# Group A of a hybrid decoder step: the values stand in the array and the softmax weights move

## The chip, the cores and the metric

The kernel runs on one core of one Trainium2 chip. The time is the device time of one launch in microseconds (us); a smaller number is better. TensorE (PE in the rows) multiplies, with its weight loads listed apart as PEld; VectorE is DVE, ScalarE is ACT, GpSimd is POOL, and SyncE (SP) issues all DMAs.

## The reference

Two layers run over 1024 prompt tokens and 8 sample tokens, in float32. Each layer projects the normalised rows with one combined matrix and splits the columns among two groups of eight heads of 64 columns. Group A is dilated window attention, group B a matrix memory. Gated feed-forward and an embedding gate follow. The change touches group A on the prompt tokens:

```
for (window, dilation) in ((128, 1), (512, 4), (2048, 16)):
    s = einsum('qhd,khd->hqk', q, k) * 64 ** -0.5      # masked to the pattern, causal
    m = max(s, axis=-1);  e = exp(s - m);  l = sum(e, axis=-1)
    o = einsum('hqk,khd->qhd', e, v) / l
merged = sum(w * o) / sum(w),   w = l * exp(m - max over patterns of m)
```

The kernel computes the three patterns as one softmax: one mask over all 1024 keys holds for each pair of tokens the logarithm of how many patterns contain it. So for each head, output = (sum over keys of e times v) / (sum over keys of e).

## The kernel before

Five engines run programs written out by hand, tied by counting semaphores. `wait_ge` on an engine holds everything that stands behind it in that engine's program.

**Group A.** The eight heads are taken as four pairs p (`PAIRS`), and each pair in 16 units u (`UNITS`, `NU`): query block qb = u // 2 of 128 tokens, and head e = u % 2 of the pair. A unit works on the keys of blocks 0 to qb. Its steps, on bank names of the PSUM tensor `ps`:

- `scores(p, qb)` (L884, TensorE, once for both heads, at odd units, one query block ahead): queries stand, keys move, a head in each half of the array's rows, into banks 0 to 3.
- `masked(p, u)` (L1692, VectorE): adds the mask, takes the row maximum and writes to one of two buffers in `att` (L1700); L1702 makes the negated maximum. It stands one unit ahead.
- `probabilities(p, u)` (L1328, ScalarE): exponential in place (L1333).
- `turn_p(p, u)` (L899, TensorE): each 128x128 block of the weights is transposed (L910) to bank 4, blocks from the fifth on to bank 5.
- `near` (L1705, VectorE, L1711) and `evac_far` (L1336, ScalarE, L1345) copy these banks to one of two further buffers in `att`. Both wait until the values of two units before have been multiplied, since the buffer alternates with the unit.
- `values(p, u)` (L913, TensorE, L923): the turned block stands, 128 keys by 128 queries, and 65 columns of `zt` move, the 64 value columns of the head and a column of ones whose product is the sum of weights. The result is 128 queries by 65 in bank 6. It stands one unit late.
- `outputs(p, u)` (L1713, VectorE): reciprocal of the 65th column (L1718), then the product into `yb` (L1719).

A float32 product is two records in the trace, a transposition one. Between these steps TensorE has `products` for the next pair's projection (L783 to L785; `FILL` gives 8 or 4 steps of three matmuls a unit, and none in units 14 and 15), and `turn_third` (L869), which transposes three tiles of normalised queries or keys through bank 6, and so waits for that bank to be read. ScalarE's `z_evac` (L1305 to L1309) takes a finished tile of products out of PSUM; in its program it stands ahead of the exponential of the same unit. VectorE normalises the next pair's queries and keys in parts (`norm_part`: L1602 to L1629), and `y_squares` adds squares of the outputs. At SP, `store_y` waits for `o_read` and stores `yb`.

Group B, the output projection, the feed-forward and the embedding gate follow, and are not touched.

## Time and profile before

| | us |
|---|---|
| runs of the kernel before | 3622.18, 3626.34, 3626.39; median 3626.34 |
| the profiled execution | 3619.83 |
| its span, first to last instruction | 3618.0 |
| TensorE busy | 3345.3 (92% of the span) |
| VectorE busy | 2166.6 (60%) |
| ScalarE busy | 883.3 (24%) |
| GpSimd busy | 597.0 (16%) |

The profile is of one execution; its own time is 6.5 us under the median of the three runs. Group A of the first layer lies between about 118 and 475 us of the span, that of the second between about 1893 and 2250 us. Where the next matmul starts before the last has ended, the distance of two starts is what one costs, and not its duration.

### The profile page before, as it was taken

How to read it: one execution, taken by the hardware profiler on the slowest of the kernel's cores; microseconds unless marked ns; L12 is line 12 of the kernel's file. 1: busy time of each engine (PE TensorE's matmuls, PEld its weight loads, DVE VectorE, ACT ScalarE, POOL GpSimd, SP SyncE). 2: the span in 40 equal slices, each digit the busy share in tenths (PEclk: the TensorE clock that was granted, in tenths of full speed). 3: DMA queues.
4: the chain of work that ended last, by engine and by line, in shares of the span. 5: the costliest groups of instructions: out<-in, count | busy, mean ns of one | idle time of the engine just before them, and what ended most of it. 6: DMA issues, size and time to landing. Idle time of an engine off the chain costs nothing. (4 is left out here: it accounts for less than half of the span.)

```text
span 3618.0 us, 49560 instructions
## 1 busy us (share of the span) xinstructions
PE 3345.3 (92%) x19817; PEld 3076.7 (85%) x19817; DVE 2166.6 (60%) x4644; ACT 883.3 (24%) x1661; POOL 597.0 (16%) x498
## 2 busy tenths in 40 slices
PE   4899999978999999999978989997899999999989
PEld 4777767668899999998977877775799999999988
DVE  5666456666655555557566665556666555555573
ACT  4233322213211211113233332232031111111131
POOL 2001111110322222221110011112012221221211
PEclk7999989959999999999989999997599999999999
DMA  4111112442211111110211111225211111111101
GB/s 141 39 36 42 42 47 74 92 134 66 70 47 36 59 47 36 59 47 18 84 41 47 45 42 51 58 64 170 73 60 36 47 47 47 47 47 47 39 30 63
DMA packets 208269, 209.69 MB, mean 58 GB/s; under 512 B 34596, under 2 KB 180964, under 8 KB 205936
## 3 DMA queue, kind: packets, MB, share of 16 engines
q1 hardware_dynamic: 208040, 206.53, 19.2%
q8 instruction: 157, 2.57, 0.3%
q14 instruction: 72, 0.59, 0.1%
HBM read 175.03 MB, written 31.64 MB: 57 GB/s over the span
## 5 line engine op out<-in xcount | busy, mean ns | idle before, releaser
L767 POOL TENSOR_TENSOR wlo<-raw,whi 128x512 fp32r<-128x512 f32 (+3 forms) x488 | 596.2, 1258 | 2964.4 <-ACT whi L1257 2964.4
L783 PE MATMUL ps<-hi,wlo 128*128 128x344 f32 x2880 | 931.8, 324 | 25.7 <-DVE wb L2077 15.5
L784 PE MATMUL ps<-lo,whi 128*128 128x344 f32 x2880 | 925.1, 321 | 0.0
L785 PE MATMUL ps<-hi,whi 128*128 128x344 f32 x2880 | 924.7, 321 | 0.0
L783 PEld LDWEIGHTS ps<-hi,wlo 128*128 128x128 f32 x2880 | 546.2, 190 | 29.0 <-DVE wb L2077 16.1
L784 PEld LDWEIGHTS ps<-lo,whi 128*128 128x128 f32 x2880 | 545.7, 189 | 0.6
L785 PEld LDWEIGHTS ps<-hi,whi 128*128 128x128 f32 x2880 | 545.8, 190 | 0.0
L783 PE MATMUL ps<-whi,lo 128*128 128x512 f32 (+5 forms) x1152 | 462.3, 401 | 40.7 <-POOL wlo L767 25.7
L784 PE MATMUL ps<-wlo,hi 128*128 128x512 f32 (+5 forms) x1152 | 436.4, 379 | 0.0
L785 PE MATMUL ps<-whi,hi 128*128 128x512 f32 (+5 forms) x1152 | 436.4, 379 | 0.0
L2089 DVE TENSOR_TENSOR X<-X,ps 128x344 f32<-128x344 f32 x528 | 268.6, 512 | 196.0 <-PE ps L785 195.4
L783 PE MATMUL ps<-yhi,wlo 128*128 128x344 f32 x1056 | 339.7, 322 | 0.6 <-DVE X L2089 0.6
L785 PE MATMUL ps<-yhi,whi 128*128 128x344 f32 x1056 | 338.3, 320 | 0.0
L784 PE MATMUL ps<-ylo,whi 128*128 128x344 f32 x1056 | 337.3, 319 | 0.0
L783 PEld LDWEIGHTS ps<-whi,lo 128*128 128x128 f32 (+1 forms) x1152 | 215.1, 187 | 119.1 <-issue 61.3
L1483 ACT ACTIVATE wb<-wb 128x344 f32<-128x344 f32 x132 | 64.9, 492 | 847.5 <-DVE wb L2060 847.5
L785 PEld LDWEIGHTS ps<-whi,hi 128*128 128x128 f32 (+1 forms) x1152 | 214.0, 186 | 39.2
L784 PEld LDWEIGHTS ps<-wlo,hi 128*128 128x128 f32 (+1 forms) x1152 | 215.7, 187 | 32.0
L1257 ACT ACTIVATE whi<-raw 128x2048 fp32r<-128x2048 f32 (+3 forms) x122 | 214.0, 1766 | 53.2 <-DMA raw<-in_w_down 41.4
L1305 ACT ACTIVATE zt<-ps,rcol 128x256 f32<-128x256 f32 x144 | 68.1, 473 | 566.5 <-PE ps L785 429.3
L783 PEld LDWEIGHTS ps<-yhi,wlo 128*128 128x128 f32 x1056 | 198.6, 188 | 1.6 <-DVE X L2089 1.2
L784 PEld LDWEIGHTS ps<-ylo,whi 128*128 128x128 f32 x1056 | 198.3, 188 | 0.0
(273 smaller groups left out, 4208.3 us busy)
## 6 DMA issues: line engine op xcount, KB each, us to landing
raw<-in_w_up SPq DMA_DIRECT2D x44, 1024.0 KB, 5.1
raw<-in_w_in SPq DMA_DIRECT2D x112, 256.0 KB, 4.6
raw<-in_w_down SPq DMA_DIRECT2D x22, 1024.0 KB, 4.9
kvb<-in_cache_win_k SPq DMA_DIRECT2D x48, 256.0 KB, 3.2
cache<-in_cache_win_v SPq DMA_DIRECT2D x36, 256.0 KB, 5.6
x_scratch<-X SPq DMA_DIRECT2D x8, 1032.0 KB, 7.2
X<-x_scratch SPq DMA_DIRECT2D x4, 2064.0 KB, 14.3
raw<-in_w_out SPq DMA_DIRECT2D x8, 1024.0 KB, 6.5
```

The source lines that it names most:

```text
L767: pool.tensor_tensor(out=wlo[:, s, r], in0=raw[:, s, r], in1=whi[:, s, r].bitcast(F32), op=ALU.subtract).then_inc(w_split, 1)
L783: nc.tensor.matmul(out, a_lo, b_hi, start=first, stop=False)
L784: nc.tensor.matmul(out, a_hi, b_lo, start=False, stop=False)
L785: return nc.tensor.matmul(out, a_hi, b_hi, start=False, stop=last)
L1257: do(nc.scalar.activation(whi[:, s, 0:used], raw[:, s, 0:used], ACT.Copy), w_hi, wait=False)
L1305: do(nc.scalar.activation(zt[0:m, z, t, 0:2 * P], src[:, 0:2 * P], ACT.Identity, scale=r), wait=False)
L1483: do(nc.scalar.activation(wb[:, col(c)], wb[:, col(c)], ACT.Gelu_apprx_tanh), gelu_done, wait=False)
L2089: do(v.tensor_tensor(out=x, in0=x, in1=ps[:, 5 + g % 3, 0:CH], op=ALU.add), dn_read, wait=False)
```

## The change

In `values(p, qb)`, now once for a query block and both heads, the 64 value columns of a head stand, head 0 in the left half of the array's columns and head 1 in the right half, and 128 columns of turned weights move. The result is turned: 64 columns of each head by 128 queries, in bank 6. `outputs_copied` on VectorE copies it to `oa` (which is the idle `Cst` buffer), `turn_back` on TensorE transposes it into the second quarter of bank 6, and `outputs` multiplies both heads by their reciprocals in one instruction. The column of ones is no longer used; the sums of weights come from the exponential's own accumulator (`accum_out`), into `dsum`.

The steps move too. `values` stands at even units behind `turn_p`, for the query block before; `turn_back` at odd units between two halves of the products, or behind `turn_p` where there are none. `turn_third` goes to the end of odd units. `near` and `evac_far` wait for the values of the query block before, both heads. The semaphores `o_ready` and `o_read` now count query blocks.

```diff
+        dsum = sb("dsum", [P, 3, 2], F32, mid)
+        oa = Cst[:, 0:P]
...
-                def values(p, u):
-                    e, qb = UNITS[u]
-                    g = NU * p + u
+                def values(p, qb):
+                    g = NU * p + 2 * qb + 1
                     pe.wait_ge(*at(pt0, g + 1))
                     if qb >= 4:
                         pe.wait_ge(*at(pt1, far(g + 1)))
-                    pe.wait_ge(*at(o_read, g))
-                    zc = VO + e * (HD + 1)
+                    pe.wait_ge(*at(o_read, NT * p + qb))
                     for kb in range(qb + 1):
-                        a = 2 * SEQ + (g % 2) * SEQ + kb * P
-                        mm = nc.tensor.matmul(ps[:, 6, 0:HD + 1], att[:, a:a + P], zt[:, p % 2, kb, zc:zc + HD + 1],
-                                              start=(kb == 0), stop=(kb == qb))
+                        for e in range(2):
+                            a = 2 * SEQ + e * SEQ + kb * P
+                            zc = VO + e * (HD + 1)
+                            mm = nc.tensor.matmul(ps[HD * e:HD * e + HD, 6, 0:P], zt[:, p % 2, kb, zc:zc + HD], att[:, a:a + P],
+                                                  start=(kb == 0), stop=(kb == qb))
                     mm.then_inc(o_ready, 1)
+                def turn_back(p, qb):
+                    pe.wait_ge(*at(oc_done, NT * p + qb + 1))
+                    nc.tensor.transpose(ps[:, 6, P:2 * P], oa[:, :], ident[:, :]).then_inc(ob_ready, 1)
...
+                        if part:
+                            evac = (q_evac, k_evac)[part[2]], 3 * part[0] + part[1] + 1
+                        before = (p, qb - 1) if qb else (p - 1, NT - 1)
                         half = (ahead(u) + ahead(u + 1)) // 2
                         products(p + 1, ahead(u), half)
-                        if part:
-                            pe.wait_ge(*at(o_read, NU * p + u - 1))
-                            turn_third(*part)
-                        products(p + 1, half, ahead(u + 1))
-                        turn_p(p, u)
-                        if part:
-                            pe.wait_ge(*at((q_evac, k_evac)[part[2]], 3 * part[0] + part[1] + 1))
-                        if u:
-                            values(p, u - 1)
-                        elif p:
-                            values(p - 1, NU - 1)
-                values(PAIRS - 1, NU - 1)
+                        if e == 0:
+                            if part:
+                                pe.wait_ge(*at(o_read, NT * p + max(qb - 1, 0)))
+                                turn_third(*part)
+                            products(p + 1, half, ahead(u + 1))
+                            turn_p(p, u)
+                            if before[0] >= 0:
+                                if part or u and turn_part(p, u - 1):
+                                    pe.wait_ge(*at(*evac))
+                                values(*before)
+                        else:
+                            if half == ahead(u + 1):
+                                turn_p(p, u)
+                            if before[0] >= 0:
+                                turn_back(*before)
+                            if half < ahead(u + 1):
+                                products(p + 1, half, ahead(u + 1))
+                                turn_p(p, u)
+                            if part:
+                                pe.wait_ge(*at(o_read, NT * p + qb))
+                                turn_third(*part)
+                values(PAIRS - 1, NT - 1)
+                turn_back(PAIRS - 1, NT - 1)
...
-                    do(nc.scalar.activation(s, s, ACT.Exp, scale=SCALE, bias=nm[:, g % 2:g % 2 + 1]), p_done, wait=False)
+                    do(nc.scalar.activation(s, s, ACT.Exp, scale=SCALE, bias=nm[:, g % 2:g % 2 + 1],
+                                             accum_out=dsum[:, g // 2 % 3, g % 2:g % 2 + 1]), p_done, wait=False)
...
-                        act.wait_ge(*at(o_ready, g - 1))
+                        act.wait_ge(*at(o_ready, NT * p + qb))
...
-                        if part and part[2] == 0:
+                        if part and part[2] == 0 and u % 2 == 0:
...
+                        if part and part[2] == 0 and u % 2:
+                            evac_third(part[0], part[1])
...
-                        dve.wait_ge(*at(o_ready, g - 1))
+                        dve.wait_ge(*at(o_ready, NT * p + UNITS[u][1]))
...
-                def outputs(p, u):
-                    e, qb = UNITS[u]
-                    dve.wait_ge(*at(o_ready, NU * p + u + 1))
-                    if u % NT == 0:
-                        dve.wait_ge(*at(yb_stored[u // NT], 16 * p))
-                    do(v.reciprocal(den[:, 1:2], ps[:, 6, HD:HD + 1]))
-                    do(v.tensor_scalar(yb[:, qb, e * HD:(e + 1) * HD], ps[:, 6, 0:HD], den[:, 1:2], None, ALU.mult), o_read)
+                def outputs_copied(p, qb):
+                    dve.wait_ge(*at(o_ready, NT * p + qb + 1))
+                    do(v.tensor_copy(oa[:, :], ps[:, 6, 0:P]), oc_done, wait=False)
+                def outputs(p, qb):
+                    if qb % 4 == 0:
+                        dve.wait_ge(*at(yb_stored[qb // 4], 16 * p))
+                    do(v.reciprocal(den[:, 0:2], dsum[:, (NT * p + qb) % 3, :]))
+                    dve.wait_ge(*at(ob_ready, NT * p + qb + 1))
+                    do(v.tensor_tensor(out=yb[:, qb, :].rearrange("p (e d) -> p e d", e=2), in0=ps[:, 6, P:2 * P].rearrange("p (e d) -> p e d", e=2),
+                                       in1=den[:, 0:2].unsqueeze(2).to_broadcast([P, 2, HD]), op=ALU.mult), o_read)
...
-                        part = turn_part(p, u)
-                        if part and part[2] == 1:
+                        part, (e, qb) = turn_part(p, u), UNITS[u]
+                        keys = part and part[2] == 1
+                        before = (p, qb - 1) if qb else (p - 1, NT - 1)
+                        if keys and e == 0:
                             evac_third(part[0], part[1])
+                        if e and before[0] >= 0:
+                            outputs(*before)
                         near(p, u)
-                        if u:
-                            outputs(p, u - 1)
-                        elif p:
-                            outputs(p - 1, NU - 1)
+                        if keys and e:
+                            evac_third(part[0], part[1])
+                        if e == 0 and before[0] >= 0:
+                            outputs_copied(*before)
...
+                outputs_copied(PAIRS - 1, NT - 1)
+                outputs(PAIRS - 1, NT - 1)
```

The remaining edits are the counts of the semaphores and the waits of `store_y`, `z_evac` and group B's first step, which now count query blocks.

TensorE at the end of the third pair, units 13 to 15, before. L910 is `turn_p`, L923 `values`, L895 `scores` of the next pair, L869 `turn_third`:

```order
L785 MATMUL ps<-whi,hi 8x384
L910 MATMUL ps<-ident,att 128x128 x7
L923 MATMUL ps<-zt,att 128x65 x7
L910 MATMUL ps<-ident,att 128x128 x8
L923 MATMUL ps<-zt,att 128x65 x7
L895 MATMUL ps<-kT,rstd 128x128 x2
L910 MATMUL ps<-ident,att 128x128 x8
L923 MATMUL ps<-zt,att 128x65 x8
L783 MATMUL ps<-whi,lo 128x512
```

The same place in the changed kernel. L913 is `turn_p`, L927 `values`, L872 `turn_third`, L898 `scores`, L934 `turn_back`:

```order
L788 MATMUL ps<-whi,hi 8x384
L913 MATMUL ps<-ident,att 128x128 x7
L872 MATMUL ps<-ident,zt 128x128 x3
L913 MATMUL ps<-ident,att 128x128 x8
L927 MATMUL ps<-att,zt 64x128 x14
L898 MATMUL ps<-kT,rstd 128x128 x2
L913 MATMUL ps<-ident,att 128x128 x8
L934 MATMUL ps<-ident,Cst 128x128
L786 MATMUL ps<-whi,lo 128x512
```

Two calls of `values` for one head (L923) have left the places behind unit 13's and unit 15's `turn_p`; `turn_third` now stands between the `turn_p` of units 13 and 14, and one call for both heads stands behind that of unit 14.

VectorE at the same place, before, from unit 14 on. L1700 and L1702 are `masked`, L1711 is `near`, L1718 and L1719 are `outputs`:

```order
L1700 ISA att,mx<-ps,mask 128x1024
L1700 ISA mx 128x1
L1702 TENSOR_SCALAR nm<-mx 128x1
L1711 COPY att<-ps 128x512
L1718 RECIPROCAL den<-ps 128x1
L1719 TENSOR_SCALAR yb<-ps,den 128x64
L1682 TENSOR_TENSOR rowr<-yb 128x512
L1686 TENSOR_REDUCE yt<-rowr 128x4
L1687 TENSOR_TENSOR ssq<-ssq,yt 128x4
L1700 ISA att,mx<-ps,mask 128x128
L1700 ISA mx 128x1
L1702 TENSOR_SCALAR nm<-mx 128x1
```

VectorE in the changed kernel, from unit 14 on. L1727 and L1729 are `masked`, L1738 is `near`, L1742 `outputs_copied`, L1748 and L1750 `outputs`:

```order
L1727 ISA att,mx<-ps,mask 128x1024
L1727 ISA mx 128x1
L1729 TENSOR_SCALAR nm<-mx 128x1
L1738 COPY att<-ps 128x512
L1742 COPY Cst<-ps 128x128
L1709 TENSOR_TENSOR rowr<-yb 128x512
L1713 TENSOR_REDUCE yt<-rowr 128x4
L1714 TENSOR_TENSOR ssq<-ssq,yt 128x4
L1727 ISA att,mx<-ps,mask 128x128
L1727 ISA mx 128x1
L1729 TENSOR_SCALAR nm<-mx 128x1
L1748 RECIPROCAL den<-dsum 128x2
```

The outputs of a unit stood behind `near`; now a copy stands there in even units, and in odd units the outputs stand ahead of `near`.

## Rows read from the trace of the kernel before

**Rows 1.** Window of group A, first layer: us, busy by engine, clock, DMA.

```profile
118.00:475.00 357.00, 327.39 (x2024) 273.98 (x2022) 217.56 (x562) 114.23 (x225) 35.87 (x32) 0.97 0.17 46
```

**Rows 2.** Timeline of TensorE, third pair's end: start, us, what.

```profile
371.91 0.93 PE L910 MATMUL ps<-ident,att 128*128 128x128 f32 x7
372.67 1.67 PE L923 MATMUL ps<-zt,att 128*128 128x65 f32 x14
374.18 1.04 PE L910 MATMUL ps<-ident,att 128*128 128x128 f32 x8
375.06 1.70 PE L923 MATMUL ps<-zt,att 128*128 128x65 f32 x14
...
377.56 1.14 PE L910 MATMUL ps<-ident,att 128*128 128x128 f32 x8 [0.38 <-ACT att L1333]
378.54 1.90 PE L923 MATMUL ps<-zt,att 128*128 128x65 f32 x16
380.25 0.47 PE L783 MATMUL ps<-whi,lo 128*128 128x512 f32 x1
```

**Rows 3.** Timeline of TensorE: transpositions among products, first layer, third pair.

```profile
344.01 0.49 PE L869 MATMUL ps<-ident,zt 128*128 128x128 f32 x3
344.26 0.42 PE L783 MATMUL ps<-whi,lo 128*128 128x384 f32 x1
344.52 0.34 PE L784 MATMUL ps<-wlo,hi 128*128 128x384 f32 x1
344.70 0.34 PE L785 MATMUL ps<-whi,hi 128*128 128x384 f32 x1
```

**Rows 4.** Timeline of TensorE in group B: half the array's columns, then all.

```profile
496.07 1.93 PE L1046 MATMUL ps<-rowr,ident 8*64 8x512 f32 x8
497.93 0.50 PE L783 MATMUL ps<-whi,lo 128*128 128x512 f32 x1
...
500.91 3.69 PE L1054 MATMUL ps<-rowr,ident 8*128 8x512 f32 x8
```

**Rows 5.** Timeline of the weight loads of the first line of rows 4.

```profile
496.98 0.14 PEld L1046 LDWEIGHTS ps<-rowr,ident 8*64 8x64 f32 x2 [0.29 <-issue]
```

**Rows 6.** Timeline of TensorE in group B: a change to half the rows and back.

```profile
512.65 0.40 PE L784 MATMUL ps<-wlo,hi 128*128 128x512 f32 x1
512.89 0.40 PE L785 MATMUL ps<-whi,hi 128*128 128x512 f32 x1
513.22 0.49 PE L1000 MATMUL ps<-rstd,kT 64*128 64x128 f32 x4
513.64 0.50 PE L783 MATMUL ps<-whi,lo 128*128 128x512 f32 x1
```

**Rows 7.** Timeline of ScalarE, third pair, unit 13.

```profile
372.11 0.47 ACT L1305 ACTIVATE zt<-ps,rcol 8x256 f32<-8x256 f32 x1 [5.22 <-PE ps L785]
...
372.86 1.15 ACT L1333 ACTIVATE att<-att,nm 128x1024 f32<-128x1024 f32 x1
```

**Rows 8.** Timeline of VectorE, third pair, unit 14.

```profile
376.25 0.69 DVE L1711 COPY att<-ps 128x512 f32<-128x512 f32 x1
```

**Rows 9.** Groups by line, shapes apart: count | busy us, mean ns | idle before.

```profile
L1719 DVE TENSOR_SCALAR yb<-ps,den 128x64 f32<-128x64 f32 x128 | 36.3, 284 | 4.5
L1885 DVE TENSOR_TENSOR yb<-ps,den 128x128 f32<-128x128 f32 x64 | 18.7, 292 | 2.2
L1711 DVE COPY att<-ps 128x128 f32<-128x128 f32 x16 | 4.7, 292 | 55.4 <-PE ps L910 55.4
L1424 ACT ACTIVATION_READ_ACCUMULATOR vectors<-vectors 64x1 f32 x2 | 0.4, 186 | 0.0
```

**Rows 10.** Waits of TensorE, 118 to 475 us: total us, times, longest.

```profile
PE ps L869 <- issue: 7.5, 5, 3.0
PE ps L895 <- DVE nm L1702: 5.3, 2, 3.5
```

**Rows 11.** Window of 3.4 us behind the longest of those waits (columns of rows 1).

```profile
163.20:166.60 3.40, 3.40 (x14) 3.30 (x14) 0.78 (x3) 0.99 (x2) 1.71 (x2) 0.50 0.46 127
```

More of the change, by code:

```diff
@@ L217 @@
     gz_abs=1, gz_ln=1, lf_done=1, gates_read=9, z_done=72, qk_norm=12, qk_ssq=12, qk_rs=12, turned=40, q_evac=20, k_evac=20,
-    s_ready=32, s_masked=64, p_done=64, t0_ready=64, t1_ready=32, pt0=64, pt1=32, o_ready=64, o_read=64,
+    s_ready=32, s_masked=64, p_done=64, t0_ready=64, t1_ready=32, pt0=64, pt1=32, o_ready=32, oc_done=32, ob_ready=32, o_read=32,
     o_exp=4, yb_done=4, yb_stored0=64, yb_stored1=112, z_stored0=384, z_stored1=384, gr_ready=1, rows_done=1, iw_done=4, gc_ready=1,
@@ L376, in build @@
             "z_done", "qk_norm", "qk_ssq", "qk_rs", "turned", "q_evac", "k_evac")]
-        s_ready, s_masked, p_done, t0_ready, t1_ready, pt0, pt1, o_ready, o_read = [sem(n) for n in (
-            "s_ready", "s_masked", "p_done", "t0_ready", "t1_ready", "pt0", "pt1", "o_ready", "o_read")]
+        s_ready, s_masked, p_done, t0_ready, t1_ready, pt0, pt1, o_ready, oc_done, ob_ready, o_read = [sem(n) for n in (
+            "s_ready", "s_masked", "p_done", "t0_ready", "t1_ready", "pt0", "pt1", "o_ready", "oc_done", "ob_ready", "o_read")]
         o_exp = sem("o_exp")
@@ L604, in store_y @@
                 def store_y(p, half):
-                    sp.wait_ge(*at(o_read, NU * p + NT * (half + 1)))
+                    sp.wait_ge(*at(o_read, NT * p + 4 * (half + 1)))
                     yv = Yd[half * 512:(half + 1) * 512, p * P:(p + 1) * P].rearrange("(t p) c -> p t c", p=P)
@@ L1024, in _ @@
                         pe.wait_ge(*at(pt1, far(NU * PAIRS)))
-                        pe.wait_ge(*at(o_read, NU * PAIRS))
+                        pe.wait_ge(*at(o_read, NT * PAIRS))
                         gate_rows()
@@ L1295, in z_evac @@
                         if p - 2 < PAIRS:
-                            act.wait_ge(*at(o_ready, NU * (p - 1)))
+                            act.wait_ge(*at(o_ready, NT * (p - 1)))
                         else:
@@ L1747, in _ @@
                             y_squares(p, rowr[:, :], slice(0, 4))
-                outputs(PAIRS - 1, NU - 1)
+                outputs_copied(PAIRS - 1, NT - 1)
+                outputs(PAIRS - 1, NT - 1)
                 y_squares(PAIRS - 1, rowr[:, :], slice(4, NT))
```

## The prediction

> **What bounds the kernel now.** I read the windows by stage first, then the timeline of TensorE inside a pair, then its waits, and last the other engines at the places where TensorE waits. In group A of the first layer TensorE is busy 327.4 of 357 us, VectorE 217.6, ScalarE 114.3, at a granted clock of 0.97 [rows 1]. So TensorE bounds the stage, but 29.6 us are idle, and where it idles another engine sets the pace. The waits name two kinds: `turn_third` for the normalised tiles (7.5 us, one of 3.0) and `scores` for the maxima (5.3 us, one of 3.5), both VectorE's work in the first half of a pair [rows 10]. In units 8 to 15 the blocks are many, and there TensorE's gaps are short.
>
> A third thing is seen only by laying two timelines beside each other. In unit 13 `turn_p` starts at 371.91 and that of unit 14 at 374.18 [rows 2]. The exponential that unit 14's needs starts at 372.86, takes 1.15 and ends at 374.01, 0.17 before; it starts so late since it stands behind the copy of the tile whose products ended just ahead of unit 13's `turn_p` [rows 7]. TensorE shows no gap there only because `values` of unit 12 fills it exactly. Work taken out of such a hole saves nothing.
>
> **What `values` costs now.** 2 layers, 4 pairs, 2 heads and 36 blocks with 2 records each are 1152 records of 65 columns. From start to the next line's start, 14 of them take 1.51 us (372.67 to 374.18) and 16 take 1.71 (378.54 to 380.25) [rows 2]: 0.107 us each. In all 123 us.
>
> **What it costs after.** A block needs two records for each head, 128 columns moving, 64 standing: again 1152 records. The question is whether the two halves run at once. The nearest rows say yes: line 1046 loads 64 columns into alternate halves and moves 512; 8 records take 1.86 us up to the next line (496.07 to 497.93), while line 1054, with all columns, takes 3.69 for 8 [rows 4]. Loads are hidden there too: the next pair's two loads take 0.14 beside the running matmuls [rows 5]. Of the 1.86, some 0.15 are loading and emptying (next part), so a step of two records is 0.43 for 512 columns and a fourth of that, 0.107, for 128; 576 steps cost 61.6 us. Saved: 61.6 us, if the halves are wholly parallel. The other end is no parallelism: 1152 times 0.107, nothing saved. I take the first, since rows 4 have the same order of instructions and the same halves; what they lack is that only 8 rows of the array are active and that both halves get the same moving data.
>
> A change of the array's shape costs something. Where products give way to the half-row form, the next start is 0.33 behind the last instead of 0.24, and the 4 records there take 0.42 (513.22 to 513.64) [rows 6], where two streams and one bare load of 0.107 make 0.32; the other 0.10 is emptying. Entering `values` therefore costs 0.10 and a bare load of half the columns, half of 0.107: 0.15, 64 times, 9.6 us. Leaving costs nothing new, as `scores`, itself in halves, stands behind it in both kernels; from halves of columns to halves of rows there is no row, between 0 and 0.2 each, and I take 0.05 (3 us), since both are already drained forms.
>
> The Trainium skill ("TensorE: Matmul & The Clock Gate", "The mechanism") says that weight loads overlap with matmuls in flight only when the row group differs. Rows 5 show loads into the same rows hidden, so I don't take it for the sum; by it every step would bare its load, which is the third rival.
>
> **`turn_back`.** 64 transpositions among products. Three such take 0.25 (344.01 to 344.26), and the product behind them 0.26 instead of 0.18 [rows 3]: one alone is 0.08 and 0.09, 0.17 us, so 10.9 us. Against it, 64 sections of old `values` at odd units go, each of which also made the product behind it 0.08 longer: 5.1 back. Gross for TensorE: 61.6 - 9.6 - 3 - 10.9 + 5.1 = 43 us.
>
> **VectorE and ScalarE.** The outputs of two units were two reciprocals and two multiplications of 0.284; now they are one reciprocal, a copy of 128 columns of 0.292 and one multiplication of 0.292 [rows 9]: about the same less one reciprocal a query block, off the path except in normalising units. There something new works the other way: `near` of an even unit waits for `values`, and its 0.4 to 0.7 us now stand behind it where they ran beside it. The reader of the accumulator costs ScalarE 0.186 [rows 9] 128 times, 24 us, hidden in its idle 240 us except where the exponential is waited for.
>
> **Where the gross saving goes.**
> - Unit 13 to 14, each pair. The hole of 2.27 us stays, as the exponential still starts behind the tile's copy; it grows by 0.19 for the reader. `values` of unit 12 (1.5) no longer fills it; `turn_third` (0.33), moved there, does in three pairs of four. Given back: 6 x 1.36 + 2 x 1.69 = 11.5 us.
> - Unit 14 to 15. `near` of unit 14 (0.69) [rows 8] starts only behind `values` (0.15 and 14 x 0.107), and unit 15's `turn_p` needs bank 4 from it: 0.88 + 1.65 + 0.69 and handovers of 0.2 are 3.42, against 3.38 now (374.18 to 377.56) [rows 2]. Where the exponential is late now, `near` is late next: nothing gained, nothing lost.
> - First halves of pairs, where VectorE and ScalarE set the pace [rows 10]: about 0.35 saved and hidden, and 0.35 added to VectorE's chain by the late `near`, in six pairs: 4 us.
> - The last pair of each layer has no products behind unit 15: `turn_back`, `outputs`, `near`, then the last `values` stand in a row, where the values of unit 14 covered `near`. 1.3 us; and copy, transposition and multiplication end the stage, 0.5 longer: 3.6 us together.
> - The clock. Behind the 3.0 us wait TensorE had the lower level, 1.2 GHz (0.50), for 3.4 us [rows 11]. One such stretch costs half its length. With new gaps of about 1 us I allow one or two more: 2 us.
>
> Sum: 43 - 11.5 - 4 - 3.6 - 2 = 22 us. The profiled execution of 3619.8 would be 3598; it stands 6.5 under the median of the runs, so from that median of 3626.3 the forecast is **3604**.
>
> **Rivals.**
> 1. More of the gross saving stays (3583 to 3593): the hole at unit 13 closes since ScalarE gets to the tile's copy earlier, or the first halves keep their savings. For it: 240 us of idle ScalarE a layer. Against: the copy waits for the products, and the order of its program is unchanged there.
> 2. Coupling goes deeper: VectorE, late in units 4 to 12 through `near` behind `values`, makes `turn_p` and `turn_back` wait, and gaps bring more clock stretches of 1.7 us. With 0.15 us more in each of 64 even units and three stretches, 9.6 + 5 us: about 3619. This is also the case that the change saves array time and no time.
> 3. The loads of halves are not hidden when the streams are as short as the loads. A bare load of 64 columns is 0.053, 576 times 31 us; 22 saved become 9 lost: 3635.
> 4. **Slower: the halves don't run at once.** With all 128 rows active, each half needs its own 128 rows of moving data, twice what any matmul of this trace reads; rows 6 run two halves of rows, which together read 128. If reads are the limit, a step costs 0.214 and the 61.6 us vanish, while changes of shape and `turn_back` stay: 3626 + 40 = 3666. It turns slower as soon as more than 22 of the 61.6 are missing, about a third of the overlap.
>
> **How the numbers follow.** Forecast (3595 to 3615) 0.60, rival 1 0.15, rival 2 0.10, rival 3 0.07, rival 4 0.08. The range of 3583 to 3625 holds the first three nearly whole and leaves out 0.17. A measurement of this kernel tells about 0.2%, 7 us, from no change. Faster by more: the forecast, rival 1 and a third of rival 2, 0.79. Within: the rest of rival 2 and a sliver of 3, 0.08. Slower: 0.13.
>
> **What would show it.** In the changed profile the 1152 records of `values` should lie in sections of 16 that take about 1.9 us, with pairs of starts some ns apart and 0.107 from pair to pair; 0.16 speaks for rival 3, 0.21 for rival 4. Unit 13's `turn_p` should again stand 2.3 to 2.5 us ahead of unit 14's, now with a gap of about a us that ends on the exponential. Unit 15's should wait for `near`. Group A should take about 10 us less a layer, nearly all of it behind unit 7 of each pair. The forecast is wrong if a stage other than group A changes, if `turn_back` shows waits for the copy, or if the clock in group A falls below 0.95.

## The result and the profile after

The changed kernel takes 3591.87 us in the median of four runs (3591.36 to 3593.18), the kernel before 3625.08 (3622.18 to 3626.39). The ratio is 0.991, with a 95% interval of 0.989 to 0.993: 33 us faster. The forecast was 3604 with a range of 3583 to 3625. The time lies inside, and 11 us more were saved than the 22 foreseen. The profiled execution took 3592.33, its span is 3589.7.

From the first start of `turn_p` to the last, group A took 333.08 us in both layers before. Now it takes 317.35 and 316.69, together 32.1 less, so the whole saving lies in group A. The spans of the two profiled executions differ by 28.3 only, since ahead of group A, where the code is the same, the changed one took 3.8 longer. The window of the first layer shows it (us, busy time of PE, PEld, DVE, ACT, POOL, clock, DMA share, GB/s), beside [rows 1]:

```profile
118.00:461.00 343.00, 310.63 (x2071) 244.16 (x2070) 201.52 (x534) 121.46 (x292) 35.56 (x32) 0.97 0.18 47
```

TensorE's busy time fell by 16.8 us there and the window by 14; the clock is the same 0.97. The timeline of TensorE at the third pair's end answers [rows 2] (start, us, what). The last three rows are the start of unit 0 of the fourth pair, with the largest section of `values`:

```profile
360.57 0.93 PE L913 MATMUL ps<-ident,att 128*128 128x128 f32 x7
361.33 0.49 PE L872 MATMUL ps<-ident,zt 128*128 128x128 f32 x3
362.81 1.09 PE L913 MATMUL ps<-ident,att 128*128 128x128 f32 x8 [0.99 <-ACT att L1357]
363.83 1.75 PE L927 MATMUL ps<-att,zt 128*64 128x128 f32 x28
365.51 0.49 PE L898 MATMUL ps<-kT,rstd 64*128 64x128 f32 x4
366.54 1.07 PE L913 MATMUL ps<-ident,att 128*128 128x128 f32 x8 [0.53 <-DVE att L1738]
367.44 0.27 PE L934 MATMUL ps<-ident,Cst 128*128 128x128 f32 x1
367.47 0.47 PE L786 MATMUL ps<-whi,lo 128*128 128x512 f32 x1
367.78 0.39 PE L787 MATMUL ps<-wlo,hi 128*128 128x512 f32 x1
...
373.12 0.27 PE L913 MATMUL ps<-ident,att 128*128 128x128 f32 x1
373.32 1.97 PE L927 MATMUL ps<-att,zt 128*64 128x128 f32 x32
375.22 0.70 PE L898 MATMUL ps<-kT,rstd 64*128 64x256 f32 x4
```

Read it in three steps. The 28 records of `values` take 1.68 us from start to the next line's start, and 32 take 1.90. Four more records, two pairs, cost 0.22, so a pair of records is 0.11, what one record cost before [rows 2]. In the trace the starts of single records lie 0.007 and 0.102 us apart in turn, 0.109 for a pair. Unit 13's `turn_p` stands 2.24 us ahead of unit 14's, where it stood 2.27, now with an open gap of 0.99 that ends on ScalarE's exponential. Unit 15's follows 3.73 behind, where it was 3.38, and ends on VectorE's `near`.

ScalarE at the same place (answering [rows 7]) still does the tile's copy before the exponential, and has the accumulator's reader behind it:

```profile
360.77 0.47 ACT L1329 ACTIVATE zt<-ps,rcol 8x256 f32<-8x256 f32 x1 [3.65 <-PE ps L788]
361.14 0.34 ACT L1333 ACTIVATE zt<-ps,rcol 8x128 f32<-8x128 f32 x1
361.51 1.15 ACT L1357 ACTIVATE att<-att,nm 128x1024 f32<-128x1024 f32 x1
362.57 0.19 ACT L1357 ACTIVATION_READ_ACCUMULATOR att<-att,nm 128x1 f32 x1
```

The waits of TensorE in group A, first layer (what waits, for whom: us in total, times, longest), answer [rows 10]:

```profile
PE ps L786 <- ACT zt L1333: 8.5, 20, 1.0
PE ps L872 <- issue: 4.9, 3, 2.2
PE ps L913 <- ACT att L1357: 4.5, 4, 1.6
PE ps L927 <- ACT zt L1345: 2.9, 1, 2.9
PE ps L913 <- DVE att L1738: 2.6, 4, 1.0
PE ps L927 <- ACT rstd L1345: 2.5, 1, 2.5
PE ps L927 <- DVE att L1738: 1.7, 1, 1.7
...
PE ps L898 <- DVE nm L1729: 0.7, 1, 0.7
PE ps L934 <- DVE Cst L1742: 0.4, 1, 0.4
```

`turn_back` (L934) waits once, for 0.4 us, in the last pair. The wait of `scores` for the maxima fell from 5.3 us [rows 10] to 0.7. New at the top are 20 waits of the products for a tile's copy (L1333). The kernel before had, in the same view:

```profile
PE ps L783 <- ACT zt L1309: 3.4, 7, 0.8
```

**Where in the pairs.** The starts of unit 0 and unit 8 split a pair. First layer, us before and after, from its 64 starts of `turn_p`:

| pair | units 0 to 7 | units 8 to the next pair |
|---|---|---|
| 1 | 42.5, 41.6 | 42.7, 38.5 |
| 2 | 43.2, 42.5 | 38.9, 35.7 |
| 3 | 46.2, 42.1 | 40.5, 37.1 |
| 4 | 45.1, 45.5 | 34.0, 34.3 (to unit 15) |

The second halves give 10.4 us, the first halves 5.3; in the second layer it is 10.4 and 6.0.

### The profile page after: what moved, and what is told of

It reads as the page before. It is cut to its first block and busy times, and to the rows that moved or that the text cites. A ratio compares the mean times of both kernels' runs of the same rounds, so it can differ in the third digit from the quotient of the medians.

```text
span 3589.7 us, 49644 instructions
## 1 busy us (share of the span) xinstructions
PE 3307.6 (92%) x19881; PEld 3014.6 (84%) x19881; DVE 2131.5 (59%) x4580; ACT 895.7 (25%) x1789; POOL 595.8 (17%) x498
## 5 line engine op out<-in xcount | busy, mean ns | idle before, releaser
L1738 DVE COPY att<-ps 128x512 f32<-128x512 f32 (+3 forms) x128 | 75.7, 592 | 220.4 <-PE ps L927 155.4
```

Source lines behind the costliest of these rows:

```text
L1738: do(v.tensor_copy(att[:, a:a + n], ps[:, 4, 0:n]), pt0, wait=False)
```

## Do the two halves run at once?

Three kernels change only what `values` does with the array. Each keeps the order of the steps of the changed kernel.

**One half of the array for both heads.**

```diff
-                    for kb in range(qb + 1):
-                        for e in range(2):
+                    for e in range(2):
+                        for kb in range(qb + 1):
...
-                            mm = nc.tensor.matmul(ps[HD * e:HD * e + HD, 6, 0:P], zt[:, p % 2, kb, zc:zc + HD], att[:, a:a + P],
+                            mm = nc.tensor.matmul(ps[0:HD, 6, 2 * P * e:2 * P * e + P], zt[:, p % 2, kb, zc:zc + HD], att[:, a:a + P],
```

> The changed kernel, but both heads' values stand in the left half of the array's columns, one head after the other, so no two streams can run at once; the outputs of the heads come out in the wrong places. Theory (the gain is that two halves stream at once, 0.107 us for a pair of records): the sections of values double, 0.107 for each record, 61.6 us more array time, of which little is hidden: 3645 to 3654 us. Rival (the halves never ran at once, the gain is from the new order of the steps): unchanged, 3590 to 3595.

It took 3653.37 us (3651.12 to 3655.31), 1.008 of the kernel before [1.0065, 1.0095]: 61.5 more than the changed kernel. Forecast for the whole overlap was 61.6. In the profiled executions 54.5 of it lie in group A and 5.0 where the code is the same, so that the two agree to a tenth is luck. TensorE's timeline, the same section of 32 records:

```profile
388.77 3.71 PE L927 MATMUL ps<-att,zt 128*64 128x128 f32 x32
392.41 0.49 PE L898 MATMUL ps<-kT,rstd 64*128 64x256 f32 x2
```

3.64 us instead of 1.90. The fourth rival (halves don't run at once) and the third (bare loads) fall with these two numbers, since 16 pairs of records at 0.21 or 0.16 make 3.4 or 2.6 us, where the changed kernel's take 1.7, and 0.2 for entering and leaving. The Trainium skill ("TensorE: Matmul & The Clock Gate", "The mechanism") says that loads overlap only where the row group differs. Here all rows are in use in both halves and the loads cost nothing beside the 0.109 of a pair; the measurement decides.

**Both halves, a head at a time.** The loops are exchanged, the halves kept:

```diff
-                    for kb in range(qb + 1):
-                        for e in range(2):
+                    for e in range(2):
+                        for kb in range(qb + 1):
```

> The changed kernel with each head in its own half, but all blocks of head 0 first and then all of head 1, where the change alternates. Theory (matmuls start in the order of the program, so two halves overlap only where neighbours differ in half): the overlap is lost but for one step a section, 0.107 for each record as with one half: 3640 to 3652 us. Rival (the queue of TensorE finds the other half's work further on): 3590 to 3600.

3635.61 us (3634.5 to 3638.24), 1.003 [1.0017, 1.004], 44 over the changed kernel and a little under the range expected of it. TensorE's timeline:

```profile
384.17 3.33 PE L927 MATMUL ps<-att,zt 128*64 128x128 f32 x32
387.43 0.70 PE L898 MATMUL ps<-kT,rstd 64*128 64x256 f32 x4
```

The section takes 3.26 us: of the 1.74 us that the halves saved, 0.38 are left. That is three and a half steps of 0.109, where the expectation had one. The sections by their number of records, us from start to the next line's start, say more:

| kernel | 4 | 8 | 12 | 16 | 32 |
|---|---|---|---|---|---|
| changed (alternating) | 0.37 | 0.59 | 0.81 | 1.02 | 1.90 |
| a head at a time | 0.37 | 0.59 | 1.07 | 1.51 | 3.26 |
| one half | 0.58 | 1.02 | 1.45 | 1.89 | 3.64 |

Up to four records of a head, nothing is lost by taking the heads in turn; beyond, 0.38 stays saved, however long the section. So in long sections the use of two halves isn't enough, and neighbours in the program should lie in different halves. But about four records of the second head do run beside the last of the first. The Trainium skill ("TensorE: Matmul & The Clock Gate", "Step-by-step: what each phase is for") says that matmuls stay in program order and only loads are pulled ahead. By a strict order of starts the halves would share one step of 0.109 in any section; from eight records on 0.38 to 0.43 are measured. The trace agrees with the page only in the main, and the measurement decides. The rows don't name the half of a record, so how the second head gets ahead is not shown.

**The new order of steps without the new product.** Weights stand and values move as before, for both heads in a row. There is no `turn_back` and no copy, and the sums come from the column of ones:

```diff
-                            mm = nc.tensor.matmul(ps[HD * e:HD * e + HD, 6, 0:P], zt[:, p % 2, kb, zc:zc + HD], att[:, a:a + P],
+                            mm = nc.tensor.matmul(ps[:, 6, P * e:P * e + HD + 1], att[:, a:a + P], zt[:, p % 2, kb, zc:zc + HD + 1],
...
-                            if before[0] >= 0:
-                                turn_back(*before)
```

> The order of the changed kernel with the arithmetic of the kernel before: turned weights stand, 65 columns move, both heads in a row at even units, no turning back, no accumulator. Theory (order alone is a loss of holes, halves are the gain): the sections double at even units, the values of unit 14 hold back the near copy by 3 us, the gap before unit 14 stays open, the queue behind VectorE in the third pair still gets shorter: 3630 to 3650 us, slower than before. Rival (the order is what helps): 3590 to 3615 us.

3645.07 us (3641.11 to 3649.03), 1.0057 [1.0042, 1.0072]. The kernel before, run beside it, took 3626.73, so the reordering by itself costs 18 us, as expected. `values` of both heads stands behind unit 14's `turn_p`, and unit 15's follows it 5.11 us behind. The new product then brings 53 us.

## The accumulator's reader

```diff
-                                             accum_out=dsum[:, g // 2 % 3, g % 2:g % 2 + 1]), p_done, wait=False)
+                                             ), p_done, wait=False)
...
+                do(v.memset(dsum[:, :, :], 1.0))
```

> The changed kernel without the exponential's accumulator; the sums are set to one, so the outputs are not divided. The forecast counted 0.19 us of the reader in the gap before unit 14's turn_p, eight times, 1.5 us. Theory now (unit 13 to 14 took 2.24 us, no longer than the 2.27 before, so the reader is not in the chain): the gap stays 0.99 us and the time 3590 to 3593. Rival (the reader is in the chain and something else got shorter): the gap falls to 0.80 and the time by 1.5 to 4 us.

3596.25 us (3593.73 to 3599.49), 0.9923 [0.9908, 0.9938]: not faster than the changed kernel, though it does less. Its time decides nothing. Its profiled execution was 6.9 us longer outside group A, where the code is the same, and in the first layer's third pair units 4 to 6 took 20.2 us instead of 19.2. Unit 13 to 14 is steadier: 2.15 us instead of 2.24 in the first three pairs of both layers, so the gap is 0.09 shorter. Neither number expected came (a gap of 0.80 or 0.99). The reader's record shows 0.19 us, but in the changed kernel ScalarE's next instruction (L1370) starts at 362.66, 0.09 behind the reader's start in the rows above, and 0.09 is what the chain lost.

## The holes in units 13 to 15 and in the fourth pair

**Products moved into unit 14.** In the fourth pair the products' tiles then end elsewhere, and unit 14 has work while it waits:

```diff
-FILL = (8, 8, 8, 4, 4, 8, 4, 4, 4, 4, 4, 4, 4, 4, 0, 0)
+FILL = (8, 8, 8, 4, 4, 4, 4, 4, 4, 4, 4, 4, 4, 4, 4, 0)
```

> The changed kernel with four of unit 5's eight steps of products moved to unit 14, so that tiles of products end in even units, ahead of the values, and unit 14 has products ahead of its turn_p. Theory (the gap of 0.99 us before unit 14's turn_p is the exponential behind the tile's copy, and the gaps of 0.4 to 1.0 in the fourth pair are products that wait for a copy which values used to cover): both kinds close, 8 us and 5 us: 3576 to 3582 us; unit 15 still waits 0.5 for the near copy. Rival (VectorE is the real limit there, so the gaps move elsewhere): 3588 to 3593 us.

3588.13 us (3586.13 to 3591.07), 0.9895 [0.9879, 0.9912], 4 us under the changed kernel where 10 to 16 were expected. The late holes closed: in the fourth pair the intervals of the odd units 5 to 11, 4.02 to 4.13 us, became 3.24 to 3.47, and the pair took 75.1 instead of 79.9. But unit 5 lost its cover in the first three pairs. TensorE's timeline, unit 5 of the first pair:

```profile
163.06 0.66 PE L872 MATMUL ps<-ident,zt 128*128 128x128 f32 x2 [5.73 <-issue]
```

`turn_third` stands there 5.7 us; the tiles that it turns come from VectorE, whose last step for them ends at 162.96. In group A the two fourth pairs won 9.6 us and the other six lost 5.6. What was won behind is lost in front.

**The same, with `values` ahead of `turn_p` in unit 14.**

```diff
-                            turn_p(p, u)
+                            if u != 14:
+                                turn_p(p, u)
...
                                 values(*before)
+                            if u == 14:
+                                turn_p(p, u)
```

> As e3_fill, and in unit 14 the values stand ahead of turn_p, so that near of unit 14 need not wait for them. Theory (unit 15's wait of 0.53 us is near behind values): it goes, 4 us, less a change of the array's shape of 0.1 to 0.2 us in each pair: 2 to 4 us under e3_fill. Rival (the wait is for the exponential as well, or leaving the halves for the whole array costs 0.3 and more): the same as e3_fill or slower.

3588.91 us (3582.18 to 3592.5), 0.9893 [0.9877, 0.9909]: no different from the one before. From unit 13 to 15 it is 6.48 us (4.95 and 1.53) against 6.85 (3.18 and 3.67), so `near` no longer holds unit 15, but 0.37 in eight places is 3 us, and the first halves varied by more.

**The exponential ahead of the tile's copy in unit 13,** nothing else:

```diff
+                        if u == 13:
+                            probabilities(p, u + 1)
                         for t in tiles(ahead(u), ahead(u + 1)):
                             z_evac(p + 1, t)
-                        if u + 1 < NU:
+                        if u == 13:
+                            pass
+                        elif u + 1 < NU:
                             probabilities(p, u + 1)
```

> The changed kernel; on ScalarE the exponential of unit 14 stands ahead of the copy of the tile in unit 13, and nothing else moves. Theory (the gap before unit 14's turn_p is ScalarE's order alone): it falls from 0.99 to 0.2 or less, 6 to 8 us: 3584 to 3586 us. Rival (the maxima from VectorE come no earlier, so the exponential can't start earlier): 3590 to 3593 us.

3586.18 us (3581.16 to 3589.25), 0.9886 [0.9871, 0.9901]: 5.7 faster than the changed kernel. Unit 13 to 14 is 1.53 in all eight pairs instead of 2.24 in six and 2.5 in the two fourth ones, 6.2 in all. TensorE's timeline of the third pair, unit 14 (L1742 is `near` in this kernel):

```profile
358.47 1.06 PE L913 MATMUL ps<-ident,att 128*128 128x128 f32 x8 [0.27 <-DVE att L1742]
```

The gap fell from 0.99 to 0.27, not quite to the 0.2 expected, and now ends on VectorE's copy of bank 4. So the hole was ScalarE's order, as the prediction read it from two timelines, and the next bound is 0.7 us behind it.

**Only what helped of these.** The exponential first in every pair's unit 13, and the moved products and `values` ahead of `turn_p` in the fourth pair alone, where no `turn_third` stands in unit 5:

```diff
+LAST = FILL[:5] + (4,) + FILL[6:14] + (4, 0)
+def ahead(u, p=0):
+    return sum((LAST if p == PAIRS - 1 else FILL)[:u])
...
+                            last = p == PAIRS - 1 and u == 14
+                            if not last:
+                                turn_p(p, u)
...
+                            if last:
+                                turn_p(p, u)
```

> The changed kernel with three edits at the ends of pairs: the exponential ahead of the tile's copy in unit 13 (all pairs), and, in the fourth pair alone, four steps of products moved from unit 5 to 14 and the values of unit 14 ahead of turn_p. Theory (each hole is of the order of two steps on one engine, and closing them where VectorE isn't late keeps the gain): 0.71 us in each of six pairs and 5 us in each fourth pair, 14 us: 3576 to 3580 us. Rival (the gaps move on): 3584 to 3592 us.

3579.65 us (3577.57 to 3581.82), 0.987 [0.9854, 0.9887], 12.2 under the changed kernel. The fourth pair takes 74.8 us instead of 79.9 and group A 308.7 and 309.2. The expectation held.

## The first halves: rounding beside the normalisation

The forecast had 4 us lost in the first halves, and they gained 11. The third pair's units 4 to 6 alone went from 23.4 to 19.2 us. VectorE's timeline of the kernel before shows why they were long:

```profile
331.11 1.71 DVE L1627 TENSOR_TENSOR rowr<-zt,rope 128x192 f32<-128x192 f32 x2
332.85 1.21 DVE L1628 TENSOR_TENSOR zt<-rowr 128x96 f32<-128x96 f32 x1
334.09 1.20 DVE L1629 TENSOR_TENSOR zt<-rowr 128x96 f32<-128x96 f32 x1
335.33 0.69 DVE L1700 CUSTOM_DVE_ANT_0 att<-ps,mask 128x512 f32<-128x512 f32 x1
```

GpSimd's timeline at the same time, the subtraction that belongs to the rounding of streamed weights:

```profile
331.12 5.29 POOL L767 TENSOR_TENSOR wlo<-raw,whi 128x512 fp32r<-128x512 f32 x4 [4.99 <-ACT whi L1257]
```

The same steps of VectorE in the changed kernel:

```profile
326.40 0.63 DVE L1654 TENSOR_TENSOR rowr<-zt,rope 128x192 f32<-128x192 f32 x2
327.06 0.26 DVE L1655 TENSOR_TENSOR zt<-rowr 128x96 f32<-128x96 f32 x1
327.36 0.26 DVE L1656 TENSOR_TENSOR zt<-rowr 128x96 f32<-128x96 f32 x1
```

and GpSimd there:

```profile
327.69 5.00 POOL L770 TENSOR_TENSOR wlo<-raw,whi 128x512 fp32r<-128x512 f32 x4 [6.55 <-ACT whi L1281]
```

Four instructions of VectorE took 4.12 us beside GpSimd and 1.15 without it; the last two are each about as long as one of GpSimd's (four in 5.29 or 5.00 us). The maxima (L1700), whose scores come from PSUM, take 0.69 us in either case. They stand behind the four, and `scores` waited 3.5 us for them [rows 10]. In the changed kernel the last of the steps ends at 327.62, and GpSimd starts at 327.69. What this near miss is worth is seen in the run without the reader. In its first layer the two did meet, on VectorE:

```profile
327.19 1.21 DVE L1655 TENSOR_TENSOR zt<-rowr 128x96 f32<-128x96 f32 x1
328.44 1.20 DVE L1656 TENSOR_TENSOR zt<-rowr 128x96 f32<-128x96 f32 x1
```

and on GpSimd:

```profile
327.01 4.98 POOL L770 TENSOR_TENSOR wlo<-raw,whi 128x512 fp32r<-128x512 f32 x4 [4.89 <-ACT whi L1281]
```

`scores` waited 2.1 us for the maxima there, with the clock at its higher level behind the wait, and units 4 to 6 took 20.2 us. In that run's second layer the two missed each other and the units took 19.2. So the meeting costs this order of steps about 1 us, and not the 4 us by which the third pair's units got shorter.

The Trainium skill ("SBUF — State Buffer", "Who interferes with whom") says that VectorE and GpSimd share a pair of ports as an exclusive lock, and that an operation of VectorE with two inputs in SBUF contends with GpSimd's reads. These rows agree with it.

Is the loss due to where the rounding stands? In the kernel before, I moved the second rounding of a pair from unit 5 to 6:

```diff
-                        if u in (3, 5):
+                        if u in (3, 6):
```

> The kernel before, with ScalarE's rounding of the second weight block one unit later (unit 6 for 5), which moves GpSimd's four subtractions with it. Theory (in the third pair the two last steps of norm_rope take 1.21 us each for 0.26, since GpSimd runs beside them, and the wait of 3.5 us for the maxima and the slow clock behind it come from that; the changed kernel gained 4.3 us there by being earlier, not by its array work): the steps take 0.26, the wait falls under 1 us, 8 to 12 us less than before: 3614 to 3618 us. Rival (VectorE is late by its own work): within 3 us of before.

3620.16 us (3616.04 to 3623.45), 0.9982 [0.9972, 0.9992]: 6 us less, somewhat under the 8 to 12 expected. In the third pair the interval from unit 6 went from 10.08 to 5.59 and in the first that from unit 5 from 7.70 to 5.26, but that from unit 8 grew from 6.16 and 6.17 to 8.17 and 8.39, and that from unit 4 of the second pair from 8.91 to 12.04 and, in the second layer, 10.49. In the third pair GpSimd now runs beside `y_squares`, whose multiplication takes 1.07 us at 337.96 for 0.68 elsewhere; behind it `values` waits 1.35 us for VectorE, and 3.4 us at the lower level of the clock follow. The collision was moved, not taken away.

Both roundings were then moved to units 11 and 12, in the changed kernel and in the kernel before:

```diff
-                        if u in (3, 5):
-                            round_block(B + 2 * (p + 2) + u // 5)
+                        if u in (11, 12):
+                            round_block(B + 2 * (p + 2) + u - 11)
```

> The changed kernel with ScalarE's two roundings of weight blocks in units 11 and 12 for 3 and 5, and GpSimd's subtractions behind them. Theory (the waits in units 4 to 8 come from these two: the rounding of 1.9 us ahead of the copy of the queries, and GpSimd's instructions of 1.25 us that hold up VectorE's small steps from 0.17 to 1.2): the waits of 2.2, 2.5, 2.9 and 0.7 us in units 4 to 7 shrink to under 0.5, and the stretches at the lower clock behind them go: 10 to 26 us less, 3566 to 3582 us. Rival (VectorE's own work in these units is the limit): within 4 us of the changed kernel's 3592.

3574.43 us (3569.1 to 3576.73), 0.9854 [0.984, 0.9869], 17.4 under the changed kernel. The waits of TensorE, first layer:

```profile
PE ps L872 <- issue: 3.7, 3, 1.4
...
PE ps L927 <- ACT rstd L1345: 1.4, 2, 1.1
PE ps L927 <- ACT zt L1345: 1.1, 1, 1.1
```

The longest waits fell from 2.9, 2.5 and 2.2 to 1.1, 1.1 and 1.4, not under 0.5 as expected. In the changed kernel this 2.9 was not GpSimd but ScalarE. Its timeline there:

```profile
314.22 1.89 ACT L1281 ACTIVATE whi<-raw 128x2048 fp32r<-128x2048 f32 x1
316.02 0.36 ACT L1345 ACTIVATE zt<-ps 128x256 f32<-128x256 f32 x1
```

The rounding (1.8 us) stands ahead of the copy that `values` waits for, and 2.9 less 1.8 is the 1.1 that is left. Behind the wait the products came 0.32 us apart instead of 0.175, at the lower level of the clock, for 3.4 us; in this kernel they don't, and group A has no such stretch in either layer. The interval of unit 4 is 7.64 instead of 10.98: 1.8 of wait and about 1.5 of clock.

The kernel before with the same edit:

> The kernel before with the same later roundings as e12_rounds_late. Theory (the waits of 3.0, 2.3 and 1.8, 2.7 and 3.5 us in units 4 to 7 come from rounding and GpSimd in the kernel before too): 20 to 30 us less than before, 3597 to 3607 us, and the distance to e12_rounds_late is then what the halves of the array are worth without these waits, about 25 to 30 us. Rival (VectorE's own work): within 4 us of before.

3606.84 us (3605.16 to 3608.31), 0.9946 [0.9931, 0.9961], 19 under the kernel before. Between these two kernels the halves are worth 32.4 us, a little over the 25 to 30 expected. The reason stands in the first pair, where the steps of VectorE in unit 11 now meet GpSimd (VectorE's timeline, then GpSimd's):

```profile
193.66 1.42 DVE L1627 TENSOR_TENSOR rowr<-zt,rope 128x192 f32<-128x192 f32 x2
195.12 0.93 DVE L1628 TENSOR_TENSOR zt<-rowr 128x96 f32<-128x96 f32 x1
196.08 0.93 DVE L1629 TENSOR_TENSOR zt<-rowr 128x96 f32<-128x96 f32 x1
```

```profile
193.73 4.15 POOL L767 TENSOR_TENSOR wlo<-raw,whi 128x384 fp32r<-128x384 f32 x4 [116.06 <-ACT whi L1257]
```

The intervals from units 11 and 12 make 16.4 and 17.3 us in the two layers there, and 12.9 in the kernel before; the changed order escapes this one too. Without these 8 us the halves and their order bring about 24.

**Both together,** the roundings in units 11 and 12 and the late units of the kernel above:

> The edits of e12_rounds_late and e13_late_units together. Theory (they are different units and different engines, so they add): the sum of the two gains under the changed kernel's 3592, 3552 to 3568 us. Rival (the later rounding fills ScalarE where the exponentials of units 12 to 14 are waited for): e12's gain only, with a gap before unit 13's or 14's turn_p.

3558.05 us (3553.43 to 3560.6), 0.981 [0.9795, 0.9825]: 33.8 under the changed kernel and 67.7 under the kernel before of the same call (3625.78). The separate gains of 17.4 and 12.2 make 29.6, so they add; in group A alone the two save 19.9 and 16.2 us, and both together 34.4. Group A takes 299.6 and 300.0 us. It is the fastest of these kernels.

## Why the prediction was right, and where not

**Mechanism and direction.** Right. A pair of records costs 0.109 where the forecast took 0.107 from half columns in group B [rows 4], and the two starts of a pair lie 0.007 us apart, the sign that it named. Taking the overlap away costs 61.5 us of the 61.6 named, the last tenth by luck. Group A fell by 15.7 and 16.4 us in the two layers, where the text had about 10, nearly all of it behind unit 7: the second halves did give 10.4 each, but the first gave the rest. And those 10.4 hold two errors that cancel, the next two paragraphs. The time lies in the band of the first rival (3583 to 3593) and outside the 3595 to 3615 of the forecast proper, which had 0.60; that it is inside the whole range is no proof of the sum.

**Changes of shape and `turn_back`: too dear.** `values` starts 0.20 behind the last transposition where 0.11 was usual, so entering costs 0.09 and not 0.15. Leaving to `scores` takes 0.20, as before: nothing, not 0.05. `turn_back` takes 0.03 of its own and makes the next product 0.08 to 0.09 longer, 0.12 and not 0.17. So 61.6 - 5.8 - 7.4 + 5.1 = 53.5 us gross, not 43. The 5.1 is the prediction's own and was not measured apart.

**The products' wait for the tile's copy: missed.** 8.5 us instead of 3.4 a layer, 10 us in all, which the sum didn't have. TensorE, fourth pair, after:

```profile
414.53 0.60 PE L913 MATMUL ps<-ident,att 128*128 128x128 f32 x4
415.77 0.50 PE L786 MATMUL ps<-whi,lo 128*128 128x512 f32 x1 [0.65 <-ACT zt L1333]
```

and ScalarE:

```profile
414.73 0.47 ACT L1329 ACTIVATE zt<-ps,rcol 128x256 f32<-128x256 f32 x1 [5.38 <-PE ps L788]
415.10 0.36 ACT L1331 ACTIVATE zt<-ps,rcol 128x128 f32<-128x128 f32 x1
415.35 0.37 ACT L1333 ACTIVATE zt<-ps,rcol 128x128 f32<-128x128 f32 x1
```

A copy of about a us follows each finished tile. Before, `turn_p` and `values` of the other head lay over it. At odd units `values` is gone, and 0.5 of `turn_p` doesn't cover a us. It is the argument that the prediction made for unit 13 ("work taken out of such a hole saves nothing"), and did not make for the other places where `values` was removed.

**Unit 13 to 14: right in the main.** 2.24 with a gap of 0.99 on the exponential, just under the 2.3 to 2.5 named. The 0.19 for the reader is not in it: the reader weighs 0.09 in the chain, and the interval did not grow at all. The run with the exponential first shows that the gap was ScalarE's order.

**Unit 14 to 15: a size off.** Nothing was to be lost; 0.35 in eight places is 2.8 us. The wait was for `near`, as named.

**First halves: wrong.** 4 us lost were foreseen, 11 gained. The prediction read the waits for VectorE [rows 10] as the length of VectorE's work, and never looked why single steps of it took 1.2 us. With the roundings moved away in both kernels, the first halves differ by only 1.8 and 1.4 us in the two layers. So about 8 of the 11 us come from the place of the roundings and are no merit of the halves; they fell out of a shift in time that nobody planned. They are nearly all in the third pair's units 4 to 6, 19.2 us for 23.4, which with the roundings away take 15.8 in the changed kernel and 16.2 in the kernel before. The step that slipped past GpSimd by 0.07 us accounts for about 1 us of these 4 a layer. Where it did meet GpSimd in the changed order, `scores` waited 2.1 us instead of 3.5 and no low stretch of the clock followed; how the other 3 us divide between the two is not shown.

**Last pair and clock.** `values` at the end waits 1.7 us for `near` and `turn_back` 0.4 for its copy, 4.2 in the two layers where 3.6 was named. Low-clock stretches of the first layer's group A make 17.0 us after and 13.6 before, one more, 1.7 us; in the second layer both kernels have the same. So the clock cost 1.7 us, where 2 were allowed.

**Rivals.** The first (more stays) holds the time in its band, and its second reason, first halves that keep their savings, is the one that held, by a cause that it didn't name. The hole at unit 13 did not close. Of the second (deeper coupling) only the last pair and unit 15 show something; `turn_back` doesn't wait in the other pairs. Its place is taken by the copy waits.

What stays open: outside group A the profiled executions differ although the code is the same. What stands ahead of it took 131.0 to 136.1 us, what lies between the two layers' group A 1441.2 to 1450.0, and what follows 1377.7 to 1386.0; why is not shown. So a difference of a few us between two kernels means little until it is found again in group A's own intervals.

## What to carry to other kernels

- Products with 64 stationary columns can go into alternate halves of the array. Let neighbours in the program alternate: a head at a time lost nothing in sections of up to eight records, but 44 of the 61 us in all.
- Before taking work out, list every place where it stood and what other engine worked under it. Each such place is a hole if that engine is then late.
- When a short step of one engine takes four times as long at some places, look at what the other engines run there before counting on its mean; moving two roundings out of the normalisation's way was worth half as much as this whole change.

## What the hardware showed that I had not expected

- VectorE's instructions of 0.17 and 0.26 us (12 and 96 columns, out of and into SBUF) take 1.20 while GpSimd runs its 1.25 us subtractions, and 0.93 beside shorter ones of 0.98. Its instructions that read PSUM take the same with and without: 0.69 for `near` and for the maxima of 512 columns.
- A shift of a few tenths of a us decides whether they meet: within one execution, without the reader, one layer's third pair met and the other's didn't, 20.2 us for 19.2.
- With all 128 rows and different moving data in each half, two float32 records of 128 columns take 0.109 us together.
- Records for the second half that stand behind all of the first half's still run beside the last of them: 0.38 us of overlap in sections of 12 to 32 records, and all of it in sections of 4 and 8.
- Entering the half-column form costs 0.09 us; going from half columns to half rows costs nothing that the rows show.
- An accumulator's reader of 0.19 us delays the next step by 0.09.
